# The eight experts of a mixture layer run in another fixed order

## The reference

```
logits = h @ router                        # (256, 8)
probs = softmax(logits)
vals, idx = top_k(probs, 2)                # equal values: the lower number first
combine = sum(one_hot(idx, 8) * (vals / sum(vals)))
for e in range(8):
    out += combine[:, e] * ((silu(h @ w_gate[e]) * (h @ w_up[e])) @ w_down[e])
```

## Time and profile before

| what | value |
|---|---|
| median of 3 runs | 1432.51 us (1428.52 to 1435.76) |
| the profiled execution's own time | 1430.54 us |
| its span | 1428.7 us |
| TensorE matmul busy | 1385.2 us (97%) |
| TensorE weight load busy | 967.0 us (68%) |
| DVE, ACT, POOL busy | 462.6, 269.0, 49.2 us |
| moved by DMA | 490.45 MB, 343 GB/s in the mean |

### The profile page before, as it was taken

How to read it: one execution, slowest core, us unless ns; L and a number is a source line. 1 busy time by engine, 2 the same in 40 slices (tenths; PEclk the granted TensorE clock), 3 DMA queues, 4 the chain that set the end, 5 groups by cost and what they waited for, 6 DMA issues and landing times.

```text
span 1428.7 us, 24611 instructions
## 1 busy us (share of the span) xinstructions
PE 1385.2 (97%) x10446; PEld 967.0 (68%) x10446; DVE 462.6 (32%) x759; ACT 269.0 (19%) x557; POOL 49.2 (3%) x63
## 2 busy tenths in 40 slices
PE   7999999999999999999999999999999999999896
PEld 4456599974698476366499954658994785664762
DVE  3587787778477241111000000111000111110112
ACT  3245321110300132111010000321000221210221
POOL 1000000000100012000000000000000000000000
PEclk9999999999999999999999999999999999999999
DMA  9977666660798689999997586999979999999995
GB/s 377 378 296 310 248 232 238 256 266 0 312 427 343 250 303 420 425 424 421 408 385 268 203 339 263 409 424 427 423 276 394 385 426 423 424 418 427 422 424 240
DMA packets 48684, 490.45 MB, mean 343 GB/s; under 512 B 7220, under 2 KB 7956, under 8 KB 14017
## 3 DMA queue, kind: packets, MB, share of 16 engines
q1 hardware_dynamic: 40288, 468.96, 80.6%
q0 software_dynamic: 6624, 17.08, 3.1%
q10 hardware_dynamic: 1664, 2.75, 0.5%
HBM read 480.83 MB, written 13.26 MB: 346 GB/s over the span
## 4 chain that ended last, share of the span: by engine, by line
PE 85%; DMA 9%; DVE 3%; ACT 1%; issue 1%; SPq 0%; ACTq 0%; DVEq 0%
PE ps L1953 24%; PE ps L1928 15%; PE ps L1995 15%; PE ps L1629 9%; DMA ring<-stream 7%; PE ps L1742 5%; PE ps L1665 4%; PE ps L1394 3%; PE ps L1576 2%; DMA hTe<-ctx_in 2%; PE ps L1911 1%; DVE acc L885 1%; PE ps L1494 1%; PE ps L1456 1%; PE ps L1510 1%
## 5 line engine op out<-in xcount | busy, mean ns | idle before, releaser
L1953 PE MATMUL ps<-ring,hTe 128*64 128x256 f32 (+1 forms) x3328 | 340.1, 383 | 10.3 <-DMA ring<-stream 6.1
L1953 PEld LDWEIGHTS ps<-ring,hTe 128*64 128x64 f32 (+1 forms) x3328 | 226.3, 131 | 104.7 <-issue 18.8
L1316 DVE TENSOR_TENSOR aT<-acc,ps 128x512 f32<-128x512 f32 x112 | 77.0, 688 | 544.7 <-ACT acc L760 544.7
L1995 PE MATMUL ps<-ring,aT 128*32 128x256 f32 (+2 forms) x1120 | 207.2, 508 | 6.4 <-DMA ring<-stream 6.3
L1928 PEld LDWEIGHTS ps<-hTe,ring 128*128 128x128 f32 x1664 | 195.1, 191 | 3.5 <-DMA ring<-stream 2.7
L1928 PE MATMUL ps<-hTe,ring 128*128 128x144 f32 (+1 forms) x1664 | 195.7, 281 | 1.8 <-DMA ring<-stream 1.8
L1995 PEld LDWEIGHTS ps<-ring,aT 128*32 128x32 f32 (+2 forms) x1120 | 81.1, 133 | 125.1 <-issue 102.2
L760 ACT ACTIVATE acc<-ps 128x512 f32<-128x512 f32 x112 | 66.9, 597 | 457.3 <-PE ps L1953 272.0
L885 DVE SCALAR_TENSOR_TENSOR acc<-ring,silu_c,acc 128x1024 f32<-128x1024 f32 x80 | 102.6, 1282 | 2.4 <-DMA ring<-stream 0.5
L1742 PE MATMUL ps<-hT,ring 128*128 128x256 f32 (+1 forms) x480 | 83.9, 337 | 0.0
L1742 PEld LDWEIGHTS ps<-hT,ring 128*128 128x128 f32 x480 | 76.2, 191 | 7.9 <-issue 0.5
(11 more groups left out here) (284 smaller groups left out, 1162.2 us busy)
## 6 DMA issues: line engine op xcount, KB each, us to landing
ring<-stream SPq DMA_DIRECT2D x174, 2048.0 KB, 14.7
ring<-stream SPq DMA_DIRECT2D x48, 1024.0 KB, 16.2
acc<-stream SPq DMA_DIRECT2D x24, 1024.0 KB, 15.5
hT<-stream SPq DMA_DIRECT2D x24, 1024.0 KB, 16.6
y_store<-aT POOLq DMA_DIRECT2D x1, 8192.0 KB, 27.8
acc<-norm_w POOLq DMA_DIRECT2D x4, 512.0 KB, 18.5
y_store<-acc ACTq DMA_DIRECT2D x10, 128.0 KB, 9.3
x<-x_in SPq DMA_DIRECT2D x1, 1024.0 KB, 5.2
```

The lines of the kernel that those rows point to most:

```text
L1316: dve.tensor_tensor(aT_e[:, u, :, :], gated_e[:, u % 2, :, :], ps[:, q:q + 2, SEQ:2 * SEQ], ALU.mult).then_inc(e_a, 1)
L1953: last = pe.matmul(to, hTe[:, k, s0:s0 + n], w, start=(k == 0), stop=(k == KD - 1))
L1995: last = pe.matmul(ps[n * r:n * (r + 1), bank, 0:cols], a_T, w[:, part * cols:(part + 1) * cols], start=(j == 0), stop=(j == NFE - 1))
```

## The change

The experts are worked on in the order of their numbers 0, 4, 3, 2, 5, 1, 6, 7 instead of 0 to 7. The host lays the expert units into `stream` in that order and permutes the router's eight columns, so that place e of the program has the logits and weights of number `EXPERT_AT[e]`. The table `above` compares the numbers, not the places, so that equal logits are ranked as in the reference. With `EXPERT_AT` = 0 to 7 it would be the same table as before. `build`, which makes the program, is not touched. The widths in the order of work become 64, 128, 64, 144, 64, 96, 96, 64.

```diff
+EXPERT_AT = (0, 4, 3, 2, 5, 1, 6, 7)
@@
-    for e in range(E):
+    for e, number in enumerate(EXPERT_AT):
         for j in range(GU_UNITS):
-            gu = gate_up(a["o_exp_gate"][0, e], a["o_exp_up"][0, e], j)
+            gu = gate_up(a["o_exp_gate"][0, number], a["o_exp_up"][0, number], j)
             stream[BASE + e * PER_EXPERT + j] = gu.transpose(2, 1, 0, 3, 4).reshape(P, UNIT)
         for j in range(NFE // 4):
-            stream[BASE + e * PER_EXPERT + GU_UNITS + j] = rows(a["o_exp_down"][0, e], j)
+            stream[BASE + e * PER_EXPERT + GU_UNITS + j] = rows(a["o_exp_down"][0, number], j)
@@
-        a["o_router"][0].reshape(KD, P, E).transpose(1, 0, 2).reshape(P, -1)], axis=1)
+        a["o_router"][0][:, list(EXPERT_AT)].reshape(KD, P, E).transpose(1, 0, 2).reshape(P, -1)], axis=1)
@@
-    above = np.stack([np.tril(np.ones((E, E)), -1), np.triu(np.ones((E, E)), 1)], axis=1).reshape(1, -1)
+    numbers = np.array(EXPERT_AT)
+    above = np.stack([numbers[None] < numbers[:, None], numbers[None] > numbers[:, None]], axis=1).reshape(1, -1)
```

## The result

The changed kernel takes 1442.74 us in the median of 7 runs (1436.82 to 1445.25), the kernel before 1431.43 us in runs beside them (1428.12 to 1435.77). The ratio is 1.0071, with a 95% interval of 1.0046 to 1.0096: slower, by about 10 us. The forecast was 1440.5 us. The profiled execution of the changed kernel took 1445.25 us (span 1443.3), the longest of its seven and 2.5 us over their median, so what follows overstates the loss by some 2.5 to 4.5 us.

The account below looks back on a forecast made before the run. The matrix engine is busy nearly throughout the experts, so only borders and the last expert can lose time. Terms 5.4 + 0.3 + 1.4 + 2.5 - 1.4 = +8.2 us on the 1432.5 median; 1440.5 us taken, range 1431 to 1449.

Parts of the forecast that it names:

- start: Before the first expert: a newly taken branch starts matmuls 3.4 us late, half clock adds 2.0; +5.4 us, bounds 3.2 to 8.7.
- first to second, with the second expert: Border 64 to 128: DMA wait stays, short jump of 0.96 us, half clock costs 2.8; +0.3 us, bounds -2.5 and +0.3.
- 128 to 64: Border after width 128: jump of 3.9 to 5.8 us hidden behind the sequencer's lead; 0, or 3 us if lead gone.
- 64 to 144: Border into width 144: new far jump exceeds the 2.0 us DMA wait by 0.9, clock 0.5; +1.4 us, bounds 0 and 4.6.
- 144 to 64: Border after width 144: jump hidden behind a lead of 6.7 to 7.2 us; 0, or 3 us if lead gone.
- 64 to 96: Border into the first width-96 expert: same as the border before expert 6 in the kernel before; no difference, 0.
- 96 to 96, with its half clock: Border between the width-96 experts: new jump, 2.0 us idle plus 0.5 for the clock; +2.5 us, bounds 0.5 and 5.3.
- 96 to 64, to the end: Last border and expert: jump hidden but weights set the end; 1.4 us stall before goes; -1.4 us, bounds -3.0 and 0.
- rival 2: Handover to the last expert: it finds a full ring and saves 15.1 us; -5.5 us in all, 1427.0; chance 0.11.
- Jumps that cost nothing: Rival at all borders: new jumps are free, targets already fetched or leads longer; about -1 us, 1431.5; chance 0.22.
- All jumps at their dearest: Rival at all borders: every jump at its highest price, each with the lower clock; +17.5 us, 1450; chance 0.11.

Follow-up runs that it names:

- B: Start jump alone: added to the kernel before (plus a jump 64b to 96a), 1435.11 us, ratio 1.0022; taken out of the changed kernel, 1441.10 us, ratio 1.0066.
- C: Straight new order, arms moved in memory for chosen jumps: before the last expert, 0.9964; also between both width-96 experts, 1.0017; at 144 to 64 and 64 to 96, 0.9972.
- B's second kernel: Changed kernel with the first expert always in arm 64a, so no start jump but a far one to 128a next: 1441.10 us, ratio 1.0066 to the kernel before.
- the straight kernel: Changed order with TensorE's eight arms written in order of work, widths constant, no tests or jumps: 1425.05 us, ratio 0.9954 to the kernel before.
- A: All tests and jumps taken out, arms in order of work: new order 1425.05 us, ratio 0.9954; old order 1429.79 us, ratio 0.9984, to the kernel before.
- the jump before the last expert in C: Straight new order with the last expert's arm between the second's and third's in memory, adding jumps at 128 to 64 and before the last: 1426.19 us, ratio 0.9964.
- D: Straight arms, expert order 0, 1, 6, 3, 4, 5, 2, 7, so width 144 comes before the last expert: 1430.82 us, ratio 0.9990 to the kernel before.
- the straight old order: The kernel before's order 0 to 7 with arms in order of work, no tests or jumps: 1429.79 us, ratio 0.9984 to the kernel before.

## Why the prediction was right, and which step failed

The sum was +8.2 us. The ratio makes it +10.2 (1432.5 times 0.0071), and the profiled executions +14.6 of span. Border by border, in the profiled executions, each expert is set against the one that the prediction set beside it (128 against 128, the 64 behind 144 against the 64 behind 144); what expert 1 took before over 119.3 us counts in the second row, as there:

| step | forecast | after minus before |
|---|---|---|
| start | +5.4 | +5.7 |
| first to second, with the second expert | +0.3 | -1.9 |
| 128 to 64 | 0 | +0.2 |
| 64 to 144 | +1.4 | +3.8 |
| 144 to 64 | 0 | **+5.3** |
| 64 to 96 | 0 | -0.2 |
| 96 to 96, with its half clock | +2.5 | +4.3 |
| 96 to 64, to the end | -1.4 | -1.1 |
| sum | +8.2 | +16.1 |

*The sum has a slip of its own.* The stall of 1.4 us at the second unit of a width-96 expert stands once before (expert 6) and once after (1.45 us in front of 1099.30, behind the border 64 to 96). The prediction took that border as unchanged, stall included, set expert 1 at 119.3 without one, and then subtracted the stall again in the last step. Counted once, its terms give 8.2 + 1.4 = +9.6 us, 1442.1 from the median.

*Start: right.* Line 2068's branch took 3.70 us for 3.46; 4.0 us more idle time, then half clock, 79.66 for 78.00. B agrees in place and size in the trace; the ratio of its runs (0.2%, 3 us) is smaller than 5.7 us, though that kernel has a second jump besides, and no run here explains it.

*First to second: right.* 0.32 us of branch, and a DMA ends the gap. The half clock cost 1.6 at width 128, not 2.8, and the gap was 1.1 shorter, within the bounds.

*64 to 144: right in kind, short in size.* The branch took 5.91 us where the mean of 4.7 was used, and ended at 833.85, 0.34 us before the matmul; the unit that the trace names as last landed at 833.53, so either would have made the engine wait, and the branch ended last. (The kernel before has two more taken branches than the earlier trace rows, 0.32 us at 715.5 and 3.74 at 1196.8; with the latter the mean is 4.5.) Half clock followed (175.56 for 173.82), which had been given a chance of a quarter; the straight kernel has the same without a jump, so these 1.7 us can't be put down to the branch. The step lies within the bound of 4.6.

*144 to 64: the step that failed.* It was forecast as "nothing, as now", because jumps of 3.9 to 5.8 us stood behind leads of 6.7 to 7.2. C shows that this holds for a branch of 5.68 us. In the changed kernel the target is another one, 64a and not 64b, and three things came together: the lead was 6.5 us (1009.75 minus 1003.26), the branch took 6.87 us, and 22 matmuls later, with no lead left, the engine stood for another 2.65 us, then half clock. The prediction did price the lost lead at 3 us but gave it no chance. The kernel before shows the same stop, though I had not read it: its has 22 matmuls behind 1326.10, which I took for a sample of the half clock, and the next line of that timeline is

```profile
1331.54 4.69 PE L1953 MATMUL ps<-ring,hTe 128*64 128x256 f32 x41 [0.95 <-issue]
```

This stop is a wait for the next instruction packet. It shows in five entries to 64a, two of them in B's second kernel; times in us:

| kernel | branch ended | matmuls went on | idle before that | packet landed |
|---|---|---|---|---|
| before | 1325.77 | 1331.54 | 0.95 | 1330.05 |
| after | 1010.13 | 1015.92 | 2.65 | 1014.55 |
| B, added | 1334.88 | 1341.48 | 1.87 | 1340.19 |
| B, taken out, behind 128 | 747.34 | 753.27 | 0.48 | 751.90 |
| B, taken out, behind 144 | 1010.00 | 1016.18 | 3.11 | 1014.74 |

The matmuls go on 5.8 to 6.6 us after the branch's end, and 1.29 to 1.50 us after the packet, about as long as a branch takes to end behind its own. Where the branch leaves over 3 us of lead, as at 1122.69 before and at 751.75 after, the 22 to 24 matmuls of 2.8 us begin late enough, and nothing is seen. So an entry to 64a from afar needs a lead of the branch plus about 3 us, and the one behind 144 had 6.5 for 9.9. In the kernel before this stop was in the last expert, where time is free.

*96 to 96: right in kind, short in size.* Branch 5.98 where the mean of 4.7 was used, idle 3.09, and half clock that cost 1.2 where a quarter of 2.0 was set; together 4.3, within the bound of 5.3. C puts the border at about 5 us against a straight one.

*Last expert: right,* and the reason too: the gap of 3.3 us is gone, and the expert takes 2.2 us longer. The first seven units for it are issued 33.1 us before it starts (1338.52 minus 1305.47), as in the earlier trace rows, though the expert before it is the second of width 96 in a row:

```profile
1181.72 28.49 SPq L413 DMA_DIRECT2D ring<-stream  x7
...
1305.47 28.49 SPq L413 DMA_DIRECT2D ring<-stream  x7
```

From that issue to the end are 126.8 us, 128.0 before. A and the jump before the last expert in C show the other half: with the jump 90.4 us behind 3.06 us of gap, without it 93.6, and the same end. Whoever counts the 3.3 us of gap as gained comes out that much too low, at +4.9 us; only a last expert at 79.7 us as well, rival 2, would turn the sign.

*The rivals.* Jumps that cost nothing: refuted, by A against the changed kernel, 1.2% in all. That was also what the Trainium skill's 108 ns for a compare-and-branch (Advanced Engine Details and Errata, Control Flow Timing) would have given; the untaken tests of 63 to 66 ns stay below it, the long branches, 3.2 to 7.0 us, are 30 to 65 times that, and the one of 0.96 us in the earlier trace rows 9 times. Full ring: refuted at this place, by D in principle. All jumps at their dearest, +17.5: the profiled execution's +14.6 is close to it, the runs' +10 lies nearer the forecast. That the sum came out within 2.3 us of the median owes much to luck: one step at 0 cost 5.3 in the trace, two jumps were 4.2 short together, a stall was subtracted twice, the second expert cost 2.2 less than forecast, and the runs lose less than the profiled execution, for which the sum would have been half of what it shows.

*What stays open.* Why a branch takes 3.2 us at one time and 7.0 at another. The difference lies before the packet starts, 0.85 us behind the branch's start at 1088.95 and 4.54 at 1003.26 in the changed kernel, with the DMA engines at a share of 1.00 both times; the packet itself took 0.9 to 1.9 us in all kernels. Why the executions with a profile of the kernels with many jumps are among the slowest of their runs (1445.25 against a median of 1442.74; 1446.09 against 1441.10), so that the table's 16.1 us are more than the runs lose. And why the second packet behind the entry of 64a comes so soon: that the entry lies close before the end of a fetched block would fit, but no run moved that arm in memory to see the stop move.

## What to carry to other kernels

Where a program jumps, its order of work and its layout in memory are one choice: the order here is 0.3 to 0.5% faster than the kernel before with the arms in line and 0.7% slower with jumps, with the same matmuls and bytes. Price a jump by the lead of the sequencer at that place, at the upper end of the branches seen and not at their mean, and look at what stands behind the entry too; a jump that is hidden by 1 us is not safe. The packets of the instruction queue say when such a wait began and ended. And a gap in front of a stretch that waits for weights is free: before counting it as a gain, ask when the last transfer is issued.

## What the runs showed of the hardware that was not expected

- A taken branch between the arms took from 0.32 to 7.03 us in these kernels, an untaken test 0.06. The Trainium skill (Runtime: NRT & Kernel Launch, Instruction fetch mechanics) has the cause, a target outside the prefetched pages; the traces agree, with a packet of 16 KB that landed 1.35 to 1.52 us before the end of each of the 40 branches over 3 us, and add the price.
- The same section calls the crossing into the next block of instructions "mostly hidden". The straight kernels, with 84 packets of that queue each, show no idle time ended by issue at a border, which agrees. Right behind a jump that used up the lead the traces show stops of 0.48 to 3.11 us, each ended 1.29 to 1.50 us after the next packet had landed.
- Of 34 idle times of 2.2 to 5.6 us inside the experts' part, up to 1370 us, 28 had 3.4 to 6.8 us at 1.2 GHz at or right behind their end, about 1.7 us lost per 3.4. The length doesn't decide it: 2.22 us before width 128 in the first kernel of C was followed by such a stretch, 3.36 us before the second expert in the straight old order was not.
